# Diffusion trunk on one core: four modulation units of the second layer go to VectorE, between the gated-linear-attention scan and the output projection's third slab, and the first MLP keeps five units a group on TensorE

## The reference

```python
def adaln(cond, w, b):                      # w: 2048 x 12288 for each layer
    m = jax.nn.silu(cond) @ w + b
    return [m.reshape(cond.shape[0], 6, 1, D_MODEL)[:, j] for j in range(6)]
...
sh1p, sc1p, g1p, sh2p, sc2p, g2p = adaln(c_ctx[None], w_ada[l], b_ada[l])
sh1s, sc1s, g1s, sh2s, sc2s, g2s = adaln(c, w_ada[l], b_ada[l])
hp = modulate(xp, norm_g[l, 0], sh1p, sc1p)            # rmsnorm(x, g) * (1 + scale) + shift
...                                                     # yp: the mixer's output @ w_o
xp = xp + g1p * rmsnorm(yp, norm_g[l, 1])
mp = sq_relu_mlp(modulate(xp, norm_g[l, 2], sh2p, sc2p), w1_mlp[l], w2_mlp[l])
xp = xp + g2p * rmsnorm(mp, norm_g[l, 3])
```

## Time and profile before

| what | value |
|---|---|
| time, median of 3 runs | 2492.58 us (2488.64 to 2493.11) |
| profiled execution | 2489.31 us, its span 2487.5 us |
| TensorE busy | 2434.9 us (98%) |
| VectorE, ScalarE, GpSimd busy | 1685.1, 1087.3, 262.6 us |
| moved by DMA | 651 MB, mean 262 GB/s |
| granted TensorE clock | 0.996 in the mean |

### The profile page before, as it was taken

The page is one execution under the profiler, slowest core; times in us unless marked ns, Lnnn a source line. Parts: engine busy times, 40 slices in busy tenths (PEclk is TensorE's granted clock), DMA queues, the critical chain, the costliest instruction groups (busy, mean ns, idle before and its releaser), DMA issues.

```text
span 2487.5 us, 37359 instructions
## 1 busy us (share of the span) xinstructions
PE 2434.9 (98%) x13794; PEld 1991.1 (80%) x13794; DVE 1685.1 (68%) x2118; ACT 1087.3 (44%) x1495; POOL 262.6 (11%) x465
## 2 busy tenths in 40 slices
PE   6899999999999999999999999999999999999998
PEld 3578888778888888888887877798888888888887
DVE  2246665587767767775568877675888678564665
ACT  3234443464333433333454456585644344343343
POOL 0021111000010010000012144200001001000000
PEclk8999999999999999999999999999999999999999
DMA  9999999969888988987877956659668668666564
GB/s 359 372 289 342 321 322 302 320 225 309 294 278 287 308 284 267 310 281 257 281 251 244 307 171 221 222 190 299 204 226 278 208 220 279 197 200 206 169 207 166
DMA packets 458056, 651.39 MB, mean 262 GB/s; under 512 B 21976, under 2 KB 316696, under 8 KB 456280
## 3 DMA queue, kind: packets, MB, share of 16 engines
q1 hardware_dynamic: 426272, 543.47, 65.6%
q0 software_dynamic: 29312, 105.12, 12.6%
q10 hardware_dynamic: 2360, 1.32, 0.2%
HBM read 634.39 MB, written 15.43 MB: 261 GB/s over the span
## 4 chain that ended last, share of the span: by engine, by line
PE 92%; DMA 3%; DVE 2%; ACT 1%; issue 1%; SPq 0%; DVEq 0%; ACTq 0%
PE PS L1380 24%; PE PS L1461 14%; PE PS L1462 14%; PE PS L1463 14%; PE PS L1383 12%; PE PS L1409 3%; DMA SCR<-in_w_ada 1%; DMA RAW<-in_w_o_na 1%; PE PS L1599 1%; PE PS L1391 1%; PE PS L1393 1%; PE PS L1392 1%; PE PS L1600 1%; PE PS L1601 1%; PE PS L1574 1%
## 5 line engine op out<-in xcount | busy, mean ns | idle before, releaser
L2002 DVE TENSOR_TENSOR WLO<-RAW,WHI 128x1024 fp32r<-128x1024 f32 x740 | 873.6, 1225 | 293.0 <-ACT WHI L1715 242.1
L1380 PE MATMUL PS<-HM,WHI 128*128 128x512 f32 x2560 | 648.4, 395 | 3.0 <-issue 2.6
L1715 ACT ACTIVATE WHI<-RAW 128x1024 fp32r<-128x1024 f32 x370 | 390.2, 1055 | 417.0 <-DMA RAW<-in_w_mlp 163.7
L1380 PEld LDWEIGHTS PS<-HM,WHI 128*128 128x128 f32 x2560 | 459.6, 189 | 101.8 <-issue 15.7
L1461 PE MATMUL PS<-WHI,HID 128*128 128x512 f32 x1152 | 450.5, 391 | 0.0
L1462 PE MATMUL PS<-WLO,HID 128*128 128x512 f32 x1152 | 448.4, 389 | 0.0
L1463 PE MATMUL PS<-WHI,HID 128*128 128x512 f32 x1152 | 448.2, 389 | 0.0
L1719 ACT ACTIVATE WHI<-RAW 128x1024 fp32r<-128x1024 f32 x370 | 388.7, 1051 | 97.4 <-DMA RAW<-in_w_mlp 65.4
L1383 PEld LDWEIGHTS PS<-HM,WLO 128*128 128x128 f32 x2560 | 348.9, 190 | 25.6
L1383 PE MATMUL PS<-HM,WLO 128*128 128x256 f32 x2560 | 356.5, 282 | 0.0
L2075 DVE SCALAR_TENSOR_TENSOR X<-X,CS 128x1024 f32<-128x1024 f32 x240 | 297.0, 1279 | 1.4 <-DMA X<-in_w_ada 0.4
(11 more groups left out here) (260 smaller groups left out, 1994.9 us busy)
## 6 DMA issues: line engine op xcount, KB each, us to landing
RAW<-in_w_mlp SPq DMA_DIRECT2D x512, 512.0 KB, 5.4
ADW<-in_w_ada SPq DMA_DIRECT2D x114, 1024.0 KB, 9.9
X<-in_w_ada POOLq DMA_DIRECT2D x224, 256.0 KB, 3.9
RAW<-in_w_qkv_na SPq DMA_DIRECT2D x68, 512.0 KB, 8.6
RAW<-in_w_qkvg_gla SPq DMA_DIRECT2D x64, 512.0 KB, 5.5
SCR<-in_w_ada SPq DMA_DIRECT2D x16, 1024.0 KB, 11.5
RAW<-in_w_o_na SPq DMA_DIRECT2D x32, 512.0 KB, 7.2
RAW<-in_w_qkvg_gla SPq DMA_DIRECT2D x64, 256.0 KB, 5.0
```

The costliest lines, as they stand in the source:

```text
L1380: return mm(bank[:, 0:2 * T2], hi[:, k, P * b:P * b + P], act[:, kc, 0:2 * T2], start=first, stop=False)
L1715: actv(WHI[:, 2 * s + u, 0:HALF], RAW[:, u, 0:HALF], ACT.Copy).then_inc(hi_half, 1)
L2002: tt(WLO[:, 2 * s + u, part], RAW[:, u, part], WHI[:, 2 * s + u, part].bitcast(f32), ALU.subtract).then_inc(done, 1)
```

## The change

The second layer's units 34 to 37 of 48 (82 to 85 in all) become a new quad `QG` on VectorE. Its 16 tiles stand in slabs 19 to 23 of the gate projection (1, 1, 1, 2, 2: `GATES_FROM`) and in slabs n = 0, 1, 2 of the output projection (3, 4, 2: `GATE_TILES`). In a gate slab they come behind the multiplies and ahead of `out_lo` and the copy-out. The two tiles in slab n = 2 come right behind its first splits. The first MLP makes five units a group on TensorE instead of six, the one in slab n = 1 falls away; the later units' numbers shift by four.

X returns only after `QG`: TensorE picks its sums behind the third quarter of slab n = 2, ScalarE stores them there, ahead of its splits of slab 3's first half, and then does the squares of x0 and x1, which wait for X, ahead of the splits of slab 3's second half. In GpSimd's queue the first 14 tiles follow the head gain; tiles 14 and 15 and X's return stand between the two halves of the post-norm gain's loads. `sum_rows` of the last slab's flush moves behind the first pair of `cross`.

```diff
-        PU = NB + 2
+        PU = NB + 1
...
-        SKIP_V = SKIP + 2 * QU
+        SKIP_V = SKIP + 3 * QU
...
-        FROM1 = QS + 1
+        QG = QS + 1
+        FROM1 = QG + 1
...
+            if f == 2:
+                parts = ("y0", "y1", "x0", "x1", "y2", "x2", "g0", "g1", "x3", "g2")
...
-        PLAN_MLP = ((0,), (1,), (), ())
+        PLAN_MLP = ((0,), (), (), ())
...
-                   (64, 80, A_WO1, QS), (80, 88, 88 - SKIP_V, FROM1), (88, A_END, A_MLP1, FROM1 + QUADS1)]
+                   (64, 80, A_WO1, QS + 1), (80, 88, 88 - SKIP_V, FROM1), (88, A_END, A_MLP1, FROM1 + QUADS1)]
...
+        GATES_FROM = {3: 1, 4: 1, 5: 1, 6: 2, 7: 2}
+        GATE_TILES = (3, 4, 2, 0)
...
                 for g in SILU.get(r, ()):
                     multiply(g)
+                for x in range(GATES_FROM.get(r - R_G, 0)):
+                    gate_tile(sum(GATES_FROM.get(q, 0) for q in range(r - R_G)) + x)
                 if r == R_G + 7:
                     out_lo(0)
                     out_lo(1)
...
-            return_x(FROM1)
             pool.wait_ge(sem("gla_qk_turned"), ITEMS)
             pool.wait_ge(sem("gla_kend"), GLA_H)
             pool.dma_start(GHEAD, g_head_gla[0:1, :].partition_broadcast(P)).then_inc(sem("ghead_in"), 16)
+            set_picks(4, PICKS)
+            for k in range(KC - 2):
+                quad_load(QG, k)
...
+                if n == 2 and x == 2:
+                    quad_rows(QG, 4, QUAD0_BANK)
...
+                if n == YN - 2 and f == 2:
+                    quad_store(QG, QUAD_UNITS[QG], QUAD0_BANK)
...
-                if 0 < n < YN - 1:
+                if 0 < n < YN - 1 and f != 2:
                     more_squares(f, (("x0",), ("x1",))[n - 1])
+                if n == YN - 2 and f == 2:
+                    more_squares(f, ("x0", "x1"))
...
-                quad_out_tile(quad, n, 0)
+                if quad is not None and out_tiles(quad)[n]:
+                    quad_out_tile(quad, n, 0)
+                    if n == 2 and f == 2:
+                        quad_out_tile(quad, n, 1)
...
+                            if x == 1 and flush is not None:
+                                sum_rows(flush)
...
-            load_gain(2)
-            park_x(3, 6)
+            load_gain(2, (0, 1))
+            for k in range(KC - 2, KC):
+                quad_load(QG, k)
+            return_x(FROM1)
+            load_gain(2, (2, 3))
+            park_x(3, 6, None)
```

More of the change, by code:

```diff
@@ L199, in build_program @@
         QUAD_UNITS = [A_WO0] + [A_MLP0 + SKIP0 + GU * g + PU for g in range(QUADS0)]
-        QUAD_UNITS += [A_WO1 + SKIP, A_WO1 + SKIP + QU, A_MLP1 + SKIP_V, A_END - QU]
+        QUAD_UNITS += [A_WO1 + SKIP + QU * q for q in range(3)] + [A_MLP1 + SKIP_V, A_END - QU]
         assert A_MLP1 + SKIP_V + 2 * QU - 1 == A_END
@@ L1089, in gla_vector, with gla_pool @@
             out_lo(3)
-        def gla_pool(pool, value_quad, quad_load, return_x):
+        def gla_pool(pool, value_quad, quad_load, set_picks):
             tt = nc.gpsimd.tensor_tensor
@@ L1267, in with_between @@
                 at = YN - 1 if plan[YN - 2] else YN - 2
-                return plan[n] + ((max(map(max, filter(None, plan))) + 1,) if n == at else ())
+                return plan[n] + ((sum(map(len, plan)),) if n == at else ())
             for n in range(YN):
@@ L2076, in quad_tile, with out_tiles @@
                 end.then_inc(quad_step, 1)
+            def out_tiles(q):
+                return GATE_TILES if isinstance(q, int) and q == QG else OUT_TILES
             def quad_out_tile(q, n, x):
                 if q is not None:
-                    k = UP_TILES + sum(OUT_TILES[:n]) + x
+                    k = KC - sum(out_tiles(q)[n:]) + x
                     quad_tile(q, k, QUAD_SLOT[k], QUAD_SLOT[:k].count(QUAD_SLOT[k]))
@@ L2088, in scan_tile, with gate_tile @@
                 quad_tile(QS, k, QUAD_SLOT[k], QUAD_SLOT[:k].count(QUAD_SLOT[k]))
+            def gate_tile(k):
+                quad_tile(QG, k, QUAD_SLOT[k], QUAD_SLOT[:k].count(QUAD_SLOT[k]))
             def value_slab(n):
@@ L2108, in out_slab @@
                     store_gain(f)
-                if flush is not None:
+                if flush is not None and n < YN - 1:
                     sum_rows(flush)
@@ L2122, in out_slab @@
                 split_lo(m + 2, 0)
-                for x in range(1, OUT_TILES[n]):
-                    quad_out_tile(quad, n, x)
+                if quad is not None:
+                    for x in range(1 if n < 2 or f != 2 else 2, out_tiles(quad)[n]):
+                        quad_out_tile(quad, n, x)
                 if flush is not None:
@@ L2365, in _ @@
                 value_slab(n)
-            gla_vector(dve, link, split_lo, evacuate, value_tile, scan_tile)
+            gla_vector(dve, link, split_lo, evacuate, value_tile, scan_tile, gate_tile)
             for n in range(YN):
-                out_slab(M_WO1, n, False, 2)
+                out_slab(M_WO1, n, False, 2, False, QG)
             both_norms(2, M_WO1, False, 1, 2, 4)
@@ L2410, in _, with load_gain @@
             pool.dma_start(FLIP, t_window[:, P:2 * P]).then_inc(sem("flip_in"), 16)
-            def load_gain(f):
-                pool.wait_ge(gain_row, f + 1)
-                pool.dma_start(gain_rows[f].rearrange("b (k n) -> k b n", k=KC), GAIN_ROW).then_inc(gain_stored, 16)
-                pool.wait_ge(gain_stored, 16 * (f + 1))
+            def load_gain(f, parts=range(YN)):
+                if 0 in parts:
+                    pool.wait_ge(gain_row, f + 1)
+                    pool.dma_start(gain_rows[f].rearrange("b (k n) -> k b n", k=KC), GAIN_ROW).then_inc(gain_stored, 16)
+                    pool.wait_ge(gain_stored, 16 * (f + 1))
                 m0 = (M_WO0, output_base(M_MLP0), M_WO1, output_base(M_MLP1))[f]
-                for n in range(YN):
+                for n in parts:
                     if n >= 2:
@@ L2444, in park_x @@
                     pool.dma_start(x_park[:, b], X[:, b, :]).then_inc(x_parked[b], 16)
-                set_picks(times + 1, picks)
+                if picks is not None:
+                    set_picks(times + 1, picks)
                 pool.wait_ge(x_parked[0], 16 * times)
@@ L2481, in value_quad @@
                     quad_load(QV, k)
-            gla_pool(pool, value_quad, quad_load, return_x)
+            gla_pool(pool, value_quad, quad_load, set_picks)
             pool.wait_ge(h_ready, 4 * 5)
```

2 lines of the change are left out of this document (1 added, 1 removed).

## The result

The changed kernel takes 2511.4 us in the median of six runs (2508.4 to 2515.2), the kernel before 2492.7 (six runs, 2488.6 to 2493.9); ratio 1.0079, 95% interval 1.0066 to 1.0092. It is slower by 18.7 us. Forecast were 2497.8 and slower; the direction came, the size lies outside the range.

What follows compares the result with a forecast made beforehand. TensorE, busy for 98% of the span, was taken to bound the kernel. The terms -8.3 + 7.8 + 7.4 = +6.9 us, added to the mean of 2490.9, gave 2497.8 us; range 2486.5 to 2506.

Steps and rivals of the forecast that it cites:

- The gain, -8.3 us: First MLP: four modulation units leave TensorE at 2.08 us each, which shows in full as 8.3 us less.
- The tail, +7.8: GLA tail: seven tiles delay copy-outs, sigmoids and products on VectorE and ScalarE, so head 3's transposes start 7.8 us later.
- the upper bound of 10: GLA tail: the most it could cost, 10 us, if slab 23's weights land 2 us later still.
- 6.7 forecast: GLA tail: TensorE's transposes of head 2 wait 6.7 us, from 1662.55, for VectorE's low part of head 0.
- rival d: TensorE's clock halves after waits; mostly hidden in the tail, but a fall in the fourth slab gives +9, 2500; chance 0.04.
- The output projection, +7.4: Output projection: pick, X's late return, squares and splits in a row move VectorE's last-slab work 7.4 us later.
- slots come free long before they are wanted: GpSimd's queue: slots free early, so tiles 14 and 15 land near 1723 and 1725 as VectorE finishes its splits.
- The third rival: Full DMA engines delay tiles 13 to 15, the reloaded weights and X by 3 to 5 us more: +11, 2502; chance 0.10.
- X lands 8.8 us after its issue: Behind the pick: X's return, issued by GpSimd at 1731.3, takes 8.8 us and is there at 1740.1.
- behind these the splits of the slab's second half: Fourth slab, ScalarE: after X's four squares, splits run 1742.6 to 1746.4; TensorE gets the third quarter 4.1 us late.

Runs made afterwards that it cites:

- e1: Against the changed kernel, the four units are left out altogether, with no tiles or pick and X returning as in the kernel before; 2482.5 us.
- e7: Changed kernel with the two tiles of the gates' last slab moved behind its copy-out, one before and one after the last product; 2508.6 us.
- e2: Changed kernel without the seven tiles in the gates' part: their loads are one row and VectorE only counts them; 2505.0 us.
- e11: Changed kernel with the nine output-projection tiles loading one row instead of 128, VectorE's work on them kept; 2510.5 us.
- e13: Changed kernel with VectorE taking tile 11 ahead of, not behind, the low parts of slab 2's first half in the output projection's slab 1; 2507.7 us.
- e17: e15 with X's return moving one partition instead of 128; 2495.2 us.
- e5: e3 with X's return moving one partition instead of 128 (16 KB for 2 MB); 2509.1 us.
- e3: Changed kernel with ScalarE rounding slab 3's first half before storing the picked row, and squaring X behind slab 3's second half; 2515.3 us.
- e15: e13 plus the reorderings of e7 and e4, all of the change still computed; 2502.0 us.
- e4: Changed kernel with GpSimd issuing tiles 14 and 15 ahead of the wait for the gain row's store and the gain's first two loads; 2509.1 us.
- e12: Changed kernel with VectorE only counting the nine output-projection tiles (22.8 us of work left out), their loads kept whole; 2505.8 us.

## Why the prediction was right in direction and wrong in size

**The gain, -8.3 us: right.** Groups are 188.07 us long, ten traces have the first MLP 8.35 us shorter, and e1 puts the timed gain at 6.7 to 13.7 us. So the cost is what was wrong: 15.2 us forecast, and after lies 28.9 us above e1.

**The tail, +7.8: right mechanism, 3.1 too small, and 0.9 above the upper bound of 10.** Tiles, copy-out, sigmoid, last product stand in one row as written down. By the rows, with 6.4 taken off, slab 23 should begin at 1650.8 and begins at 1652.14; the copy-out ends 1.8 us late. The other 1.3 are the clock: behind the 8.33 us wait (6.7 forecast) the granted clock is 0.50 (1.2 GHz) from 1664.5 to 1670, eight transposes take 1.94 us instead of 1.03, and a quarter of slab 0 is slowed so that it, and not VectorE's product (done at 1672.4), holds head 3's transposes until 1673.88. The prediction priced this clock (rival d) and set it aside as hidden here. e7 and e2 show the row of waits: two tiles moved behind the copy-out take 4.9 us off TensorE's wait.

**The output projection, +7.4: wrong, 18.5.** It splits at the pick. The prediction has it at 1729.9, with the 4.55 us by which head 3's transposes shifted at 1734.45; it comes at 1740.29, 5.8 us late. From pick to sum of squares it has 27.2 us (1729.9 to 1757.1); it takes 32.5, 5.3 more. 7.4 + 5.8 + 5.3 is 18.5.

The step that failed ahead of the pick is the sentence on GpSimd's queue: "slots come free long before they are wanted", with tiles 14 and 15 landing near 1723 and 1725. I had laid out VectorE's work per slab, and not the loop step, slot free, issue, landing. Slab 1 wants four tiles with three of them in a row, from two slots; the load of the fourth can go out only when the second is done, and it takes 6.8 us. GpSimd waits for that slot in its queue, and with it the gain row's store, its 5.8 us, four gain loads and tiles 14 and 15. That this wait is there and what ends it is shown: eleven traces have it, also with single rows to load (e11), and it is gone in all five where tile 11 is taken sooner (e13 to e17).

It is not the whole 5.8. From head 3's transposes to the pick the prediction has 60.6 us and after takes 66.4; e13, with tile 13's wait gone, takes 63.9, and the rest stands behind weights that come late. The third rival, full DMA engines delaying tiles 13 to 15, the weights and X, named these places, and its 2502 is the nearest of the forecasts, though 9 us short. A tile's own bytes hardly matter for when it lands (e11). Whether they make the weights late isn't shown: no run has e13's order and e11's bytes together. The lull at 1665 to 1680 (DMA share 0.17) I read as the same loop from the other side, without a run of its own: VectorE stands still for the sigmoid, no slot comes free, no weight is reloaded, and then all is wanted at once (share 0.94 from 1680 to 1715, 0.97 from 1715 to 1740).

The Trainium skill (DMA: Bandwidth & Descriptors, "Issuing engines are not separate DMA queues") has transfers of different engines interleave on the same 16 DMA engines. e5 and e17 agree: without the bytes of X, which GpSimd issues, SyncE's weights land after 7.2 to 8.8 us instead of 11.2 to 15.0 (e5 against e3) and 5.2 to 5.8 instead of 6.9 to 10.7 (e17 against e15). The time falls by 6.2 and 6.8 us; in e17 ScalarE's squares, which no longer wait long for X, have a part in that.

Behind the pick the row on ScalarE was right piece by piece: X lands 8.8 us after its issue, as forecast, and four squares follow. The step that failed here is "behind these the splits of the slab's second half", priced at ScalarE's own time alone, as if the weights were there. They aren't: the second half is issued at 1746 to 1750, as VectorE takes the low parts of the first, 4 to 7 us behind X's 2 MB, with the gain's 1 MB in between, and lands 9.6 to 11.7 us later; ScalarE waits another 2.26 + 1.79 + 0.5 us. The picking matmuls at half clock (granted 0.50 over 1740.0 to 1742.2; 1.93 us instead of 1.07) are 0.9. e3 shows that ScalarE's order is not the bound, and e5 and e17 that X's bytes are most of it. The interval from pick to sum of squares is 31.3 to 32.9 us in all nine traces with after's order there (after, e2, e4, e7, e11 to e15), whatever came ahead; without X's bytes it is 26.6 (e17), and in e3's order 29.4 instead of 35.6 (e5 against e3).

**The second MLP's first group, +1.6: chance.** Its first eight matmuls take 3.39 us, in the trace of before 2.09. The clock was back at 1.00 from 1767 to 1793 and fell again, to 0.50 from 1794 to 1796, behind a stretch with short waits (TensorE busy for 4.10 of 6.00 us). Among the changed kernels only e7 has this too; the other sixteen have the group as long as before.

**What stays open.** The sum of 24.6 is 6 us more than the medians differ. In after's profiled execution 1.6 of them are this fall of the clock and 2.0 the waits in the first MLP; which of the other waits were long by chance can't be told. Why a load of one row takes 7 to 8 us (order in the engines' queues, or the issue itself on GpSimd) was not separated.

## What to carry to other kernels

For work fed through a ring of two slots, lay out the loop (last use, issue, landing, next use), not only the sum of busy times: a landing of 7 us allows two steps of 2.5 us in a row, not three, and the engine that issues the loads carries everything behind them in its queue. Spread the steps before making them cheaper: e12, without any of the nine steps, still waits for the loads. And before moving a big transfer into a stage, look at what is issued within a landing time behind it: an edit that only reorders the waits there shows a shorter wait in one row and a longer one in the next, and the time stays.

## What the runs showed of the hardware

- With the DMA engines at 0.97, in e11 at about 0.8, the time from issue to use hardly depended on size: 6.8 and 8.2 us for 4 KB, 6.8 and 8.4 us for 512 KB (one execution each).
- 2 MB issued by GpSimd 2 to 5 us ahead of SyncE's four loads of 512 KB lengthened these from 7.2 to 8.8 us to 11.2 to 15.0.
- The granted clock was 0.50 behind a wait of 8.33 us, and 0.77 in the mean over 1740 to 1765, where TensorE had waited 4.46 and then 6.42 us. The picking matmuls behind a wait of 1.80 us (e7) ran at the full 1.07 us, those behind 4.46 us at 1.93. In between, the wait's length didn't decide: behind 3.43 us (e7) the eight transposes took 1.94 us, behind 3.45 (e17) 1.06; the pick took 1.93 behind 3.96 us (e17) and 1.40 behind 4.65 (e3).
